# Causal attention in a two-block kernel: the short tile of each pair goes ahead of the long one, and the heads are prepared in the other pair of score banks

## The reference, cut to what matters

```
DILATED_PATTERNS = ((128, 1), (512, 4), (2048, 16))

def dilated_attention_branch(qkv, gate, q_norm_w, k_norm_w, rel_bias):
    ...
    for window, dilation in DILATED_PATTERNS:
        o_p, lse_p = dilated_pattern(q, k, v, rel_bias, window, dilation)
        outs.append(o_p)
        lses.append(lse_p)
    wts = jax.nn.softmax(jnp.stack(lses), axis=0)
    o = jnp.sum(wts[..., None] * jnp.stack(outs), axis=0)
    o = o.transpose(0, 2, 1, 3).reshape(bsz, s, D_ATT)
    return o * jax.nn.silu(gate.astype(jnp.float32))
```

## Time and profile before

| | |
|---|---|
| median of 3 runs | 1440.15 us (1439.24 to 1440.4) |
| the profiled execution | 1439.33 us, of which the span is 1437.5 us |
| six middle heads of the attention | 96.58 us, from 1226.37 to 1322.95 us |

### The profile page before, as it was taken

How to read it: one execution, slowest core, us unless ns; L and a number is a source line. 1 busy time by engine, 2 the same in 40 slices (tenths; PEclk the granted TensorE clock), 3 DMA queues, 4 the chain that set the end, 5 groups by cost and what they waited for, 6 DMA issues and landing times.

```text
span 1437.5 us, 30581 instructions
## 1 busy us (share of the span) xinstructions
PE 1392.8 (97%) x12346; PEld 1227.2 (85%) x12346; DVE 986.9 (69%) x1616; ACT 652.0 (45%) x1262; POOL 585.3 (41%) x603
## 2 busy tenths in 40 slices
PE   7999999989999999999998999999998998999998
PEld 6998899977887788888898998888997887888887
DVE  6887888689999788645684227973606776888431
ACT  6332133277777577533543221322335554777200
POOL 0168676440000477431218572212107884334420
PEclk9999999999999999999999999999999999999999
DMA  7104333180000322354654415431121121222342
GB/s 258 42 3 131 97 109 117 60 188 1 1 1 1 114 73 74 117 192 153 109 144 72 106 16 113 49 59 30 30 88 33 28 88 53 74 69 63 107 135 82
DMA packets 98259, 117.89 MB, mean 82 GB/s; under 512 B 25727, under 2 KB 79647, under 8 KB 98120
## 3 DMA queue, kind: packets, MB, share of 16 engines
q1 hardware_dynamic: 98120, 115.94, 29.8%
HBM read 86.49 MB, written 29.41 MB: 81 GB/s over the span
## 4 chain that ended last, share of the span: by engine, by line
PE 56%; DVE 7%; issue 2%; ACT 1%; POOL 0%; DVEq 0%; ACTq 0%
PE ps L407 13%; PE ps L2003 12%; PE ps L925 7%; PE ps L3611 2%; PE ps L1803 2%; PE ps L1787 2%; PE ps L3597 2%; PE ps L2987 1%; PE ps L2930 1%; PE ps L3586 1%; PE ps L2945 1%; PE ps L1780 1%; PE ps L1781 1%; PE ps L1782 1%; PE ps L3574 1%
## 5 line engine op out<-in xcount | busy, mean ns | idle before, releaser
L734 POOL TENSOR_TENSOR p_w_lo<-p_w_raw,p_w_hi 128x1024 fp32r<-128x1024 f32 x40 | 102.8, 2577 | 99.9 <-ACT p_w_hi L730 99.9
L373 POOL TENSOR_TENSOR p_w_lo<-p_w_raw,p_w_hi 128x2048 fp32r<-128x2048 f32 (+1 forms) x11 | 53.3, 4842 | 219.0 <-ACT p_w_hi L346 219.0
L963 DVE TENSOR_TENSOR tok<-tok,ps 128x512 f32<-128x512 f32 x50 | 34.2, 686 | 91.9 <-PE ps L925 77.4
L730 ACT CAST p_w_hi<-p_w_raw 128x1024 fp32r<-128x1024 f32 x40 | 41.8, 1048 | 117.4 <-POOL p_w_raw L738 76.2
L1500 DVE TENSOR_TENSOR a_pt_lo<-ps,a_pt_hi 128x512 fp32r<-128x512 f32 x128 | 82.1, 683 | 14.6 <-ACT a_pt_hi L1554 14.6
L1554 ACT CAST a_pt_hi<-ps 128x512 fp32r<-128x512 f32 x128 | 68.9, 590 | 46.2 <-PE ps L1437 46.2
L925 PE MATMUL ps<-p_w_hi,f_s_b 128*128 128x256 f32 x288 | 81.3, 282 | 2.8 <-issue 2.8
L925 PE MATMUL ps<-p_w_hi,f_s_a 128*128 128x256 f32 x288 | 81.4, 283 | 0.0
L1488 DVE TENSOR_REDUCE a_stat<-ps 128x1 f32<-128x1024 f32 x64 | 77.7, 1214 | 0.6 <-PE ps L1424 0.6
L407 PE MATMUL ps<-w_out_hi,p_w_hi 128*128 128x512 f32 x192 | 76.2, 397 | 0.5 <-DVE tok L963 0.5
L1546 ACT ACTIVATE tok<-ps,a_stat 128x1024 f32<-128x1024 f32 x64 | 72.4, 1132 | 8.6 <-DVE a_stat L1488 8.6
(11 more groups left out here) (376 smaller groups left out, 4834.8 us busy)
## 6 DMA issues: line engine op xcount, KB each, us to landing
p_w_raw<-w_in SPq DMA_DIRECT2D x20, 512.0 KB, 5.0
p_w_raw<-w_in SPq DMA_DIRECT2D x9, 1024.0 KB, 8.8
f_raw<-w_in SPq DMA_DIRECT2D x16, 512.0 KB, 4.8
kbT<-x SPq DMA_DIRECT2D x8, 512.0 KB, 6.8
b_w_raw<-w_out SPq DMA_DIRECT2D x8, 512.0 KB, 3.7
qT<-s_gate SPq DMA_DIRECT2D x8, 512.0 KB, 6.1
qT<-x SPq DMA_DIRECT2D x8, 512.0 KB, 3.7
s_x<-qT SPq DMA_DIRECT2D x8, 512.0 KB, 2.6
```

The costliest lines, as they stand in the source:

```text
L373: ops.tensor_tensor(self.w_lo[:, b, :, 0:w], self.raw[:, :, 0:w], self.w_hi[:, b, :, 0:w].bitcast(F32), ALU.subtract).then_inc(self.w_lo_r ...
L730: self.nc.scalar.copy(self.slot(self.pr.w_hi, n), self.raw[self.source[i]]).then_inc(self.hi_ready, 1)
L734: self.nc.gpsimd.tensor_tensor(self.slot(self.pr.w_lo, n), self.raw[self.source[n % 7]], self.slot(self.pr.w_hi, n).bitcast(F32), ALU.subt ...
```

## The change

Three lines are changed. The order within each pair of tiles is turned round. The bank in which heads are prepared becomes bank 1, because now the short tiles have the even units and with them banks 0 and 1, of which they use bank 0. And the rule which engine copies a short tile's probabilities names the tiles 1 and 3 themselves, so that the same tiles are VectorE's as before.

```
-ORDER = (7, 0, 6, 1, 5, 2, 4, 3)
+ORDER = (0, 7, 1, 6, 2, 5, 3, 4)
...
-    PREP_BANK = 3
+    PREP_BANK = 1
...
     def emptier(u, piece):
-        return "dve" if piece == 1 or u % 4 == 3 else "act"
+        return "dve" if piece == 1 or units[u][1] in (1, 3) else "act"
```

## The result

The changed kernel takes 1461.48 us (median; 1460.41 to 1463.49), the one before 1440.01 us (median of four runs): a ratio of 1.0153, 95% interval 1.014 to 1.0165. The profiled execution has a span of 1459.3 us, 21.8 us more than before. Slower was forecast, at 1460.5 us, for the four waits that the changed kernel shows.

A forecast was written before the change was run, and what follows sets the result against it. In-order TensorE, busy 97%, was taken as the bound. Six middle heads 17.3, first 1.0 and last 1.9 us summed to 20.2 us on 1439.33 us; with 0.8 us for the median, 1460.5 us was predicted, range 1452 to 1466 us.

The forecast's parts named there:

- the four waits: TensorE standing still at positions 0, 2, 4 and 6 of a middle head: 3.34 us against 0.45 us before.
- value block at position 2: Longest tile's values wait for VectorE's store behind a low part: 2.68 us chain, 1.30 us work between, 1.38 us wait.
- fourth preparation: Preparing transposes at position 4 wait for VectorE's low part of position 3: 0.94 us in place of 0.45 us.
- transposes at positions 0 and 6: Transposes wait until ScalarE has copied out their bank: 1.44 us chain, 0.93 us work between, 0.51 us wait each.
- a middle head: One of six heads with preparations in the causal attention: about 19.0 us instead of 16.10 us.
- six middle heads more: Added time of the six heads with preparations, 2.89 us each: 17.3 us.
- first head more: Added time of the head that starts the attention: +1.0 us, between -1 and +2.9 us.
- last head more: Added time of the head without preparations: +1.9 us, between +0.5 and +2.9 us.
- The range: 1452 us if semaphore chains are some 0.3 us shorter; 1466 us if longer, first and last heads at upper ends.
- The one in which the wait ahead of the fourth preparation simply goes: Faster rival: the 0.45 us wait a head goes and no other forms, 1436 us; 4%.
- The smaller one: Rival: only the two chains through VectorE cost, bank waits are covered; 1.87 us a head, 1453 us; 10%.
- the 1474 us of that rival: Larger rival: TensorE's clock falls, each head losing 1.7 us, 14 us on top of the forecast; 5%.

## Why the prediction was right, point by point

| step | predicted | measured |
|---|---|---|
| value block at position 2 | 1.38 us | 1.28 us |
| fourth preparation | 0.94 us | 0.91 us |
| transposes at positions 0 and 6 | 0.51 us each | 0.59 and 0.49 us |
| a middle head | 19.0 us | 19.13 us |
| six middle heads more | 17.3 us | 18.2 us (114.76 - 96.58) |
| first head more | 1.0 us | 0.6 us, where the third scores of the second head start (1226.37, now 1226.97) |
| last head more | 1.9 us | 2.9 us |
| median | 1460.5 us | 1461.48 us |

*The value block.* The mechanism was the one written down, with the same order on VectorE (high part, low part, store, values), and taking the store out of the queue takes 0.97 us of the 1.28 us away. The 0.31 us that is left belongs to that edit, whose second store makes the copy later; in the changed kernel the copy was done 1.31 us before the store.

*The fourth preparation.* Size and cause were right. What I had not seen is that the wait for the store at position 4 lies right behind it, so that it can't be saved alone.

*The banks.* Both are there, and covering them with values makes them vanish. The sizes came out near in part by luck. At position 0 the chain from the five transposes to the next use of the bank is 1.56 us (1264.63 to 1266.19 us), not 1.44 us, with 0.97 us of work in it, not 0.93 us. At position 6 both are shorter than predicted: 1.39 us (1260.64 to 1262.03 us) and 0.90 us.

*The middle heads* lost 3.27 us to the four waits, where 3.34 us were predicted. The head is longer than these waits and the work explain: 15.61 us, the head without such waits, and 3.27 us make 18.9 us. The remaining 0.25 us is some 0.06 us for each stop, and most of it is a matter of counting. Lengths go from start to start, and one weight load begins before the record of the one ahead has ended: a score's of 0.19 us is followed after 0.14 us when nothing waits (1260.50 to 1260.64 us). A wait in the brackets is counted only from the end of that record.

*The last head* is the term that was too small, by 1.0 us. The timeline of the changed kernel in that head, first positions 2 and 4, then its end:

```profile
1346.46 0.20 PEld L3597 LDWEIGHTS ps<-ident,c_prob 128*128 128x128 f32 x2 [0.27 <-issue]
...
1347.53 1.04 PEld L3611 LDWEIGHTS ps<-c_v,c_prob_t 128*64 128x64 f32 x32 [0.51 <-issue]
...
1350.78 0.31 PEld L3597 LDWEIGHTS ps<-ident,c_prob 128*128 128x128 f32 x3 [0.38 <-issue]
...
1355.98 1.38 DVE L3914 TENSOR_TENSOR c_table<-tok,c_raw 128x512 f32<-128x512 f32 x1
...
1357.47 0.28 DVE L3686 TENSOR_SCALAR tok<-ps,c_stat 128x64 f32<-128x64 f32 x1
...
1357.87 0.58 PEld L3611 LDWEIGHTS ps<-c_v,c_prob_t 128*64 128x64 f32 x16 [0.88 <-issue]
...
1362.00 0.19 PEld L2003 LDWEIGHTS ps<-w_out_hi,c_q_hi 128*128 128x128 f32 x1 [0.87 <-DVE c_q_lo L2034]
```

The values of the last short tile wait 0.88 us for a store that stands behind the gating of the output's second tile (L3914, 1.38 us). My sum for the last head had left that instruction out. It had also left out two bank waits, 0.27 us at position 2 and 0.38 us at position 4: the cover that I had counted for these positions has a preparation in it, and the last head prepares nothing. Against these 1.53 us stands the long tile's value block, which waits 0.51 us where I had 0.98 us, so the term missed by less than its parts. From the third scores of the last head to the output projection it is 20.27 us (1341.73 to 1362.00) where it was 17.35 us (1322.95 to 1340.30).

*The range.* Its upper end does not follow from its own words: 0.3 us more for each of four waits in six heads, with the first and last head at their upper ends, makes 1470.6 us and not 1466 us. The measured time lies below either.

*The rivals.* The one in which the wait ahead of the fourth preparation simply goes did not come, as the chain was 2.68 us against 1.30 us of work; its saving is real, but in the other order, by moving the preparations (1436.13 us). The smaller one (only the chains through VectorE) fails on the bank waits that the trace shows. The clock did not fall: it reads 1.00 over the whole stage, with four stops of 0.5 to 1.3 us in every 19 us. The fall in the earlier trace rows did not follow the gap as directly as the prediction has it: between the 2 us with little work and the stretch at 0.50 lies one from 1082 to 1084 us, not among those rows, at 1.00 with 1.53 us busy. In what these traces show the cycling through PSUM banks, which the Trainium skill names, from another kernel, as a cause of a swinging clock ("TensorE: Matmul & The Clock Gate", section "A second HAM failure mode: psum-queue depth-cycling"), did not cost any clock here; the 1474 us of that rival were not seen.

## What to carry to other kernels

When an in-order engine is nearly full, ask of every wait how much of its own work lies between the producer and the consumer, and compare that with the whole chain through the other engines: here 1.30 us stood against 2.68 us. Turning a pair round keeps all work and all dependencies and only changes that distance, and with TensorE busy nearly all of the time each missing piece of cover was paid in full here: 3.27 us of visible waits in a head that became 3.03 us longer and had lost a wait of 0.45 us. A wait that is removed alone may uncover one of the same length behind it, so look up what is queued behind the same instruction on the engine that is waited for, as the store was behind the low part.

## What the runs showed of the hardware

TensorE's weight loads start 0.05 to 0.12 us after the end of the VectorE or ScalarE instruction that they wait for, in the rows shown here. A value block starts with 0.17 us of idle time ahead of its weight loads even when no producer is late, in the order of before as in the one that is fastest, four times a head; I had counted it as given, and no run shows where it comes from. Waits in the brackets of the weight loads come out some 0.06 us too short for each stop, since successive weight loads overlap.
